# A fifth slot for the first feed-forward piece, filled within the output product

## The reference

```
proj   = x @ w_in[l]                          # three attentions and their gates
merged = sum_i gates_i * (out_i @ w_branch[l, i])
mix    = merged @ w_out[l]                    # "the output product", 1024 x 1024
x      = layer_norm(ALPHA * x + mix, ln1_g, ln1_b)
gu     = x @ w_ffn_in[l]                      # 1024 x (2 * 2816)
hidden = silu(gu[..., :2816]) * gu[..., 2816:]
x      = layer_norm(ALPHA * x + hidden @ w_ffn_out[l], ln2_g, ln2_b)
```

## Time and profile before

| | us |
|---|---|
| median of 3 runs | 1446.25 |
| the profiled execution's own time | 1446.09 |
| its span | 1444.8 |
| PE busy in it | 1432.1 |
| DVE busy in it | 1040.6 |
| ACT busy in it | 820.3 |

### The profile page before, as it was taken

How to read it: one execution, slowest core, us unless ns; L and a number is a source line. 1 busy time by engine, 2 the same in 40 slices (tenths; PEclk the granted TensorE clock), 3 DMA queues, 4 the chain that set the end, 5 groups by cost and what they waited for, 6 DMA issues and landing times.

```text
span 1444.8 us, 19800 instructions
## 1 busy us (share of the span) xinstructions
PE 1432.1 (99%) x7753; PEld 1208.5 (84%) x7753; DVE 1040.6 (72%) x1423; ACT 820.3 (57%) x1193; POOL 58.9 (4%) x100
## 2 busy tenths in 40 slices
PE   8999999999999999999999999999999999999999
PEld 6888878888888888887888888888888888888888
DVE  5766976755567566875865557777988868788886
ACT  5565664454453565764455445686655657775563
POOL 1000000000001000000100000200000012000000
PEclk9999999999999999999999999999999999999999
DMA  8754635575665464642866566336566644456651
GB/s 272 250 191 148 220 130 174 173 236 185 201 206 170 152 212 126 216 148 91 253 211 221 185 203 204 98 110 202 175 200 196 211 139 156 147 174 203 198 182 59
DMA packets 172686, 261.11 MB, mean 181 GB/s; under 512 B 9521, under 2 KB 111569, under 8 KB 172337
## 3 DMA queue, kind: packets, MB, share of 16 engines
q1 hardware_dynamic: 171296, 255.18, 54.4%
q0 software_dynamic: 1152, 4.65, 1.0%
q10 hardware_dynamic: 144, 0.01, 0.0%
HBM read 256.66 MB, written 1.05 MB: 178 GB/s over the span
## 4 chain that ended last, share of the span: by engine, by line
PE 93%; DVE 5%; ACT 1%; issue 1%; POOL 0%; DMA 0%; DVEq 0%; ACTq 0%
PE ps L500 16%; PE ps L575 12%; PE ps L577 11%; PE ps L576 11%; PE ps L501 9%; PE ps L470 7%; PE ps L474 7%; PE ps L472 7%; PE ps L503 2%; DVE wlo L1770 1%; PE ps L1121 1%; PE ps L528 1%; PE ps L618 1%; PE ps L1101 1%; PE ps L629 1%
## 5 line engine op out<-in xcount | busy, mean ns | idle before, releaser
L1770 DVE TENSOR_TENSOR wlo<-raw,whi 128x2048 fp32r<-128x2048 f32 (+3 forms) x230 | 510.2, 2227 | 223.0 <-ACT whi L1237 223.0
L1237 ACT ACTIVATE whi<-raw 128x2048 fp32r<-128x2048 f32 (+3 forms) x230 | 426.9, 1866 | 124.3 <-PE ps L577 51.7
L500 PE MATMUL ps<-xT,whi 128*128 128x512 f32 x1008 | 356.4, 395 | 0.0
L501 PE MATMUL ps<-xT,wlo 128*128 128x256 f32 x1152 | 311.3, 280 | 0.0
L575 PE MATMUL ps<-whi,xT 128*128 128x512 f32 (+3 forms) x640 | 250.1, 391 | 1.5 <-DVE xT L1848 1.0
L577 PE MATMUL ps<-whi,xT 128*128 128x512 f32 (+3 forms) x640 | 242.1, 378 | 0.0
L576 PE MATMUL ps<-wlo,xT 128*128 128x512 f32 (+3 forms) x640 | 241.3, 377 | 0.0
L500 PEld LDWEIGHTS ps<-xT,whi 128*128 128x128 f32 x1008 | 189.0, 188 | 42.1
L501 PEld LDWEIGHTS ps<-xT,wlo 128*128 128x128 f32 x1152 | 217.4, 189 | 6.1
L575 PEld LDWEIGHTS ps<-whi,xT 128*128 128x128 f32 x640 | 120.3, 188 | 23.5 <-issue 4.5
L577 PEld LDWEIGHTS ps<-whi,xT 128*128 128x128 f32 x640 | 120.2, 188 | 22.6
(11 more groups left out here) (264 smaller groups left out, 2026.9 us busy)
## 6 DMA issues: line engine op xcount, KB each, us to landing
raw<-in_w_in SPq DMA_DIRECT2D x120, 512.0 KB, 4.7
raw<-in_w_ffn_in SPq DMA_DIRECT2D x88, 512.0 KB, 4.9
raw<-in_w_up SPq DMA_DIRECT2D x88, 512.0 KB, 4.8
raw<-in_w_ffn_out SPq DMA_DIRECT2D x44, 512.0 KB, 4.5
raw<-in_w_down SPq DMA_DIRECT2D x44, 512.0 KB, 4.6
raw<-in_w_branch SPq DMA_DIRECT2D x24, 512.0 KB, 4.8
raw<-in_w_out SPq DMA_DIRECT2D x16, 512.0 KB, 4.5
raw<-in_w_o SPq DMA_DIRECT2D x16, 512.0 KB, 4.5
```

Of the source, the lines that this page charges most:

```text
L500: PE.matmul(ps[:, b, :], hi, m.xT[:, kt], start=kt == 0, stop=False)
L501: mm = PE.matmul(ps[:, b, 0:S], lo, m.xTh[:, kt], start=False, stop=False)
L1237: AC.activation(weights_of(k, i)[0][:, 0:w], m.raw[:, slot, 0:w], ACT.Copy).then_inc(s.w_hi, 1)
L1770: DV.tensor_tensor(lo[:, 0:w], m.raw[:, slot, 0:w], hi[:, 0:w].bitcast(F32), ALU.subtract).then_inc(s.w_lo, 1)
```

## The change

The pair aside in `proj`'s memory, number `SPLIT`, also takes F0 in both layers of the first stack. F0 then waits for no piece of the output product. ACT rounds it right after the last high part of the turned merged gates, and DVE subtracts it between half A and half B; before, ACT rounded it when W0 had been used up and DVE subtracted it behind half C. F1 takes the pair that W0 leaves, where before it was F0, and so on: F1 to F4 each find their pair one piece earlier. The `ahead` counts around it are changed so that both engines still hold the same pieces in the same order. SP's program is the same, instruction for instruction, and so is PE's, but for the tiles that F0's matmuls read.

```diff
--- before.py
+++ after.py
@@ -150,6 +150,7 @@
 def rounding_slots(pieces, first):
 
     aside = {first[1, L, "dn", NSTEP - 3 + i]: SPLIT + i for L in range(DEPTH) for i in range(2)}
+    aside.update({first[1, L, "up", 0]: SPLIT for L in range(DEPTH)})
     slots, last, turn = [], {}, 0
     for i in range(pieces):
         slot = aside.get(i, turn % SPLIT)
@@ -1531,9 +1532,9 @@
         split_to(w0 + 4)
         turn_hi_quarter(1, 1, 0.5)
         up0 = k.first[1, L, "up", 0]
-        for i in (3, 4):
-            catch(1, L, "w", i)
-        catch(1, L, "w", 5)
+        split_to(up0 + 1)
+        for i in (3, 4, 5):
+            catch(1, L, "w", i, ahead=SPLIT + 1)
         turn_hi(0)
         catch(1, L, "w", 6)
 
@@ -2209,10 +2210,11 @@
         split_to(w0 + 4)
         catch(1, L, "w", 3)
         up0 = k.first[1, L, "up", 0]
+        split_to(up0 + 1)
         catch(1, L, "w", 4)
         DV.wait_ge(s.ln_in, 32 * (L + 1))
         apply(0)
-        catch(1, L, "w", 5, ahead=SPLIT - 1)
+        catch(1, L, "w", 5)
         turn_lo(0)
         split_to(up0 + 2)
         catch(1, L, "w", 6, ahead=0)
```

## The result

The changed kernel's median is 1449.17 us in 22 runs (1447.5 to 1450.41), against 1446.55 for the kernel before on the same chip (22 runs, 1446.21 to 1447.38). The ratio is 1.0016, with a 95% interval of 1.0011 to 1.0022: 2.6 us slower by the medians, where +1.6 was forecast. The single times stand in two groups: 7 of the 22 lie from 1447.5 to 1448.3, with a median of 1447.97, and 14 from 1449.04 to 1449.65 with one at 1450.41, these 15 with a median of 1449.25. Between 1448.3 and 1449.0 there is none. The times of before show no such gap.

A forecast was written before the change was run, and what follows sets the result against it. PE, busy 99% of the span, was taken to bound the kernel. Layer 0's -0.37 and layer 1's +1.99 (stall 2.53, gain 0.54) gave +1.6 on 1446.09, 1447.7; with the median 0.16 above, 1447.9 us, range 1445.2 to 1449.2.

The forecast's parts named there:

- the second rival: Half D, layer 1: PE's stall halves the clock for matmuls behind it; +3.3 us, sum +4.9, 1451.2 us; chance 0.09.
- if the clock falls: Sign of being wrong: PEclk was to stay at 1.00 between 710 and 730 us, in layer 1.
- The mechanism of the stall: Layer 1: F0 lands late, half B is added at 708.74, `apply(0)` is 3.69 us late, PE waits at its transposes.
- layer 0: F0's subtraction fits DVE's 2.44 us hole, half D is added 0.74 us earlier, PE goes on earlier: 0.37 us won.
- stall of PE in half D, layer 1: PE waits for `apply(0)` before both fours of transposes, so half D ends 2.53 us later; bounds 1.3 to 2.6.
- gain at `apply(1)`, layer 1: `apply(1)` comes 0.71 us nearer to PE, whose first transposes then do not wait: a gain of 0.54 us.
- No wait inside the trace let the clock fall: Argument against the clock falling in layer 1: no wait inside the program had lowered the clock in the earlier trace.
- the four transposes split the stall: Argument against the clock falling in half D, layer 1: four transposes divide the stall into 1.4 and 1.1 us.
- F3's load: Issued earlier, once F0's subtraction is done; ACT, not PE, waited for it, so nothing was taken for it.
- No stall: Layer 1: F0 lands in time or PE's slack takes the delay; both layers win, -0.9, 1445.3 us; chance 0.08.
- The hole of layer 0: Rival that DVE's hole does not hold F0's subtraction, so the 0.37 gain goes: +2.0, 1448.3 us; chance 0.08.
- The extra slot: It helps in places taken for covered, or the change fails its aim: -2 to 0, 1444.3 to 1446.3 us; chance 0.07.

The follow-up runs named there:

- the loads behind F2: The full change, with layer 1's three loads of the other stack's parameters issued after F2's load instead of ahead of F0's: 1445.46 us, again 1445.35, ratio 0.9992 of before.
- layer 1 alone: The change made in layer 1 only, layer 0 as in the kernel before: 1449.91 us, ratio 1.0020 of before.

## Why the prediction was right, and where it was not

**The time.** 1449.17 lies inside the range (1445.2 to 1449.2) by 0.03 us, and that is luck: the range was drawn to leave out most of the second rival, and by the groups it was the second rival that came in most runs, cheaper than priced. The change is slower by 0.16% where 0.11% was forecast. The forecast of 1447.9 is the time of the lower group, 1447.97: the case taken as the likeliest was worked out rightly, and it was not the likeliest. The prediction had named "if the clock falls" as a sign of being wrong, and that sign came.

**The mechanism of the stall** came as worked out, place by place: F0's rounding waits for its load and starts at 704.13 (704.6 forecast), its subtraction at 706.08 (706.5), half B is added at 708.29 (708.7), the eight transposes fall into two fours with 1.18 and 0.79 us of idle time (1.2 and 0.9). The waits for that line sum to 2.0 us and not 2.5. One reading was incomplete: the prediction puts F0's late landing down to the three loads ahead of it; with the loads behind F2, an earlier issue was 2.5 us of what F0 gained (2.5 of 3.2 in the first profile), and nearly half of those 2.5 was SP's wait for the merged gates.

**The terms**, by the profiled execution, in us:

| term | forecast | measured |
|---|---|---|
| layer 0 | -0.37 | -0.41 |
| stall of PE in half D, layer 1 | +2.53 | +2.41 |
| slow transposes and matmuls, lower clock | not in the sum | +1.51 |
| gain at `apply(1)`, layer 1 | -0.54 | -0.59 |

The stall: the second four transposes could have ended at 712.44 - 0.43 = 712.01 and end at 714.02 + 0.40 = 714.42 at the full clock. The slow work: from 714.42 to half D's end there are 4.21 us before, which gives 718.63, and the next stage starts at 720.14. The gain: 7.37 us from there to the matmul of 724.02 before, 6.78 after. With 0.02 of drift between the layers the four are the 2.90 us by which the matmul at 726.92 is late.

**The step that failed** is the weight of rival 2, "the stall brings the clock down", with a chance of 0.09 and a price of +3.3. By the groups the clock fell in 15 of 22 runs, and in 7 of 11 with layer 1 alone. Two arguments led there. "No wait inside the trace let the clock fall" was weak evidence, since the longest wait of PE behind the start was 1.0 us, in the view of the earlier trace rows:

```profile
PE ps L575 <- DVE xT L1848: 1.0, 1, 1.0
```
And "the four transposes split the stall" held nothing off: the clock fell between the two fours. The earlier trace rows had shown a fall 2.1 us after PE's last instruction, and the forecast stall was 2.5; in my judgement that should have had an even chance. The price was too high by a factor of two: +3.3 lay between a slow stretch as long as the stall (+2.5) and all 18 matmuls of half D (+4.1), and six of them were slow, 0.43 us apart and not 0.46, beside the second four transposes. The groups lie 1.3 us apart (1.8 with layer 1 alone), the traces have 1.5 and 1.6. With PE kept busy the stall stayed and the slow work went. The Trainium skill (TensorE: Matmul & The Clock Gate, section "The HAM clock gate") says that the throttled clock is the default and activity releases it; these runs agree.

**F3's load** I had taken as worth nothing. It is worth nothing where F3 lands as in the profile before, and 0.8 us (by the distances) where it lands 1.5 us later.

**The other rivals.** No stall (0.08): the stall was there, and is gone only with F0's load ahead of the parameters. The hole of layer 0 (0.08) held, with 0.25 us to spare. The extra slot (0.07) did nothing elsewhere that I could find.

## What to carry to other kernels

A free slot lets work move forward only where its data is there: before an instruction is moved into a hole of an engine, read the landing of its load in each repetition of the loop, since the same hole was right in layer 0, while in layer 1 it made everything behind it 3.7 us late. If it is too early, look at what stands ahead of that load in its queue, waits included; here a wait and three loads that nobody needed soon were in the way, and with them behind, the same edit wins some 1.0 us. When a change makes TensorE stand still, price a fall of its clock too (here +1.3 to +1.8 us in most runs) and not only the wait.

## What the runs showed of the hardware

The clock's answer to a stall is not the same in each run of one program: with a stall of 2.4 us in two parts it fell in about two runs of three (15 of 22 and 7 of 11, by the groups; in both profiled executions by PEclk), and with 3.7 us in two parts by the times in at least seven of nine, but not in the execution that was profiled. A fall cost 1.5 and 1.6 us in the two traces that have one, and 1.3 and 1.8 us by the distance of the groups. Transposes of the identity, eleven and nine or eight and six, kept the clock at 2.4 GHz in the profiles, and left one group of times.

The time of a load to its landing is not fixed by its place in the queue: with the parameters behind F2, F0's second load took 6.9 us in one profile and 5.1 in the other of the same kernel.
